# A 512-column pass for the high weight half in the feed-forward stage, with sums on drain and gate products on GpSimd

## The reference

```python
def _conv_ffn(h, w_up, conv_w, conv_b, w_down):        # D_MODEL 1024, D_FF 2816
    a, g = jnp.split(h @ w_up, 2, axis=-1)             # w_up 1024 x 5632
    a = causal_depthwise_conv(a, conv_w, width 3) + conv_b
    return (jax.nn.gelu(a) * g) @ w_down               # w_down 2816 x 1024
# and around it, in first_block:
h = _rmsnorm(x, norm_g[l, 2]) * (1.0 + sc2) + sh2
y = _conv_ffn(h, ...)
x = x + g2 * _rmsnorm(y, norm_g[l, 3])
```

## Time and profile before

| what | value |
|---|---|
| executions | 752.69, 753.12 and 759.79 us, median 753.12 |
| profiled execution | span 757.1 us; no other time of this execution is given |
| mean granted TensorE clock | 0.990 |
| TensorE busy, matmul and weight load | 730.8 us (97%) and 710.5 us (94%) |
| VectorE, ScalarE, GpSimd busy | 524.7, 396.1, 104.3 us |
| DMA | 141.13 MB, mean 186 GB/s |
| up chunks | 239.6 to 364.4 us of the span |
| down chunks | 364.4 to 426.7 us of the span |

### The profile page before, as it was taken

How to read it: one execution, slowest core, us unless ns; L and a number is a source line. 1 busy time by engine, 2 the same in 40 slices (tenths; PEclk the granted TensorE clock), 3 DMA queues, 4 the chain that set the end, 5 groups by cost and what they waited for, 6 DMA issues and landing times.

```text
span 757.1 us, 14222 instructions
## 1 busy us (share of the span) xinstructions
PE 730.8 (97%) x5964; PEld 710.5 (94%) x5964; DVE 524.7 (69%) x778; ACT 396.1 (52%) x560; POOL 104.3 (14%) x87
## 2 busy tenths in 40 slices
PE   8899999998899999999999999999999999999995
PEld 6799899898898999999999989899999999999995
DVE  4979888886977678777767556925576347555665
ACT  4286455545364544544544348528555456556551
POOL 0130000000522000000001130000004455443000
PEclk9999999999999999999999999979999999999998
DMA  8995567555363455654566544514446553343101
GB/s 343 411 356 190 203 268 274 193 204 219 113 244 146 167 200 190 213 178 161 204 261 233 205 138 148 207 66 168 167 154 223 184 206 117 116 159 112 57 1 56
DMA packets 22265, 141.13 MB, mean 186 GB/s; under 512 B 2389, under 2 KB 3029, under 8 KB 6458
## 3 DMA queue, kind: packets, MB, share of 16 engines
q1 hardware_dynamic: 21626, 137.28, 50.1%
q0 software_dynamic: 576, 2.95, 1.0%
HBM read 139.17 MB, written 1.05 MB: 185 GB/s over the span
## 4 chain that ended last, share of the span: by engine, by line
PE 70%; DVE 13%; issue 7%; ACT 5%; DMA 3%; POOL 0%; SPq 0%; DVEq 0%; ACTq 0%
PE res L1596 20%; PE res L1598 19%; PE res L1597 19%; ACT whi L639 3%; DVE wlo L1052 3%; PE pX L1803 2%; DMA shared<-in_w_ada 1%; PE pS L1783 1%; PE pX L1982 1%; DVE shared L1065 1%; DVE raw L1065 1%; DMA y<-in_w_ada 1%; ACT sq L654 1%; PE pT L1793 1%; PE pS L1644 1%
## 5 line engine op out<-in xcount | busy, mean ns | idle before, releaser
L1596 PE MATMUL res<-hhi,whi 128*128 128x256 f32 (+1 forms) x1120 | 318.9, 285 | 4.1 <-DVE wlo L1052 1.5
L1052 DVE TENSOR_TENSOR wlo<-raw,whi 128x2048 fp32r<-128x2048 f32 (+3 forms) x101 | 229.1, 2270 | 126.4 <-ACT whi L639 126.2
L1597 PE MATMUL res<-hhi,wlo 128*128 128x256 f32 (+1 forms) x1120 | 312.9, 279 | 0.0
L1598 PE MATMUL res<-hlo,whi 128*128 128x256 f32 (+1 forms) x1120 | 312.8, 279 | 0.0
L639 ACT ACTIVATE whi<-raw 128x2048 fp32r<-128x2048 f32 (+3 forms) x101 | 188.3, 1865 | 120.2 <-issue 87.1
L1596 PEld LDWEIGHTS res<-hhi,whi 128*128 128x128 f32 (+1 forms) x1120 | 209.6, 187 | 5.9 <-issue 3.4
L1597 PEld LDWEIGHTS res<-hhi,wlo 128*128 128x128 f32 (+1 forms) x1120 | 209.4, 187 | 0.4
L1598 PEld LDWEIGHTS res<-hlo,whi 128*128 128x128 f32 (+1 forms) x1120 | 209.4, 187 | 0.2
L538 POOL TENSOR_TENSOR sq<-sq,rope 128x512 f32<-128x512 f32 x18 | 39.5, 2195 | 78.5 <-ACT sq L654 78.5
L1596 PE MATMUL res<-uhi,whi 128*128 128x256 f32 x176 | 49.3, 280 | 0.0
L1597 PE MATMUL res<-uhi,wlo 128*128 128x256 f32 x176 | 49.1, 279 | 0.0
(11 more groups left out here) (334 smaller groups left out, 1211.1 us busy)
## 6 DMA issues: line engine op xcount, KB each, us to landing
raw<-in_wts SPq DMA_DIRECT2D x97, 1024.0 KB, 5.0
raw<-in_w_ada SPq DMA_DIRECT2D x16, 1024.0 KB, 5.1
shared<-in_w_ada SPq DMA_DIRECT2D x6, 1024.0 KB, 11.1
gates<-in_wts SPq DMA_DIRECT2D x4, 768.0 KB, 13.3
raw<-in_wts SPq DMA_DIRECT2D x4, 768.0 KB, 5.6
y<-in_w_ada SPq DMA_DIRECT2D x2, 1024.0 KB, 9.2
x<-in_xT SPq DMA_DIRECT2D x2, 512.0 KB, 4.7
gv<-in_ln_rows POOLq DMA_DIRECT2D x1, 1024.0 KB, 7.5
```

What stands on the lines that cost most here:

```text
L1052: nc.vector.tensor_tensor(lo[:, 0:b], raw[RAW_OF["w", c] % RAW][:, 0:b], hi[:, 0:b].bitcast(f32), ALU.subtract).then_inc(lo_ready, 1)
L1596: mm(out, ah, bh, start=first, stop=False)
L1597: mm(out, al, bh, start=False, stop=False)
L1598: return mm(out, ah, bl, start=False, stop=last)
```

## The change

Four things are changed, and all belong to the feed-forward stage.

- `hhi` and `hlo` become the two halves of one tile `hh` of [128, 8, 2, 256], and `uhi` and `ulo` those of `uh`. High and low of a k-tile lie side by side. `side_by_side` issues one matmul of the high weights with all 512 columns, and one of the low weights with the 256 high columns. The result has two parts of 256 columns for each half `i`, in two banks for a chunk. There are three such pairs of banks: `pT`, `res0` with `res1`, and `pS`. The last half of the last down block keeps `three`.
- The two parts are added on drain: ScalarE copies one part to SBUF ahead of `high`, and VectorE adds the other from PSUM ahead of `low`.
- The gate product and the subtraction for `ulo` move from VectorE to GpSimd. The rounding to `uhi` moves one iteration later on ScalarE, behind the next `high`.
- `turned` ahead of `UP + 2` is left out.

```diff
-        hhi = sb("hhi", [P, KT, T], f32r)
-        hlo = sb("hlo", [P, KT, T], f32r)
+        hh = sb("hh", [P, KT, 2, T], f32r)
+        hhi, hlo = hh[:, :, 0, :], hh[:, :, 1, :]
...
+        pairs = (pT[:, :].rearrange("p (a b) -> p a b", a=2), banks[:, 0:2, :], pS[:, :].rearrange("p (a b) -> p a b", a=2))
...
@@ GpSimd, iteration c
+                if UP <= c - 1 < DOWN and (c - 1 - UP) % 2 == 1:
+                    j = (c - 1 - UP) // 2
+                    g = gelu[:, j % 2, :, :]
+                    pool.wait_ge(gelu_done, j + 1)
+                    pool.wait_ge(drained_dve, RESULT_DRAIN[FIRST_RESULT[c - 1]][1])
+                    nc.gpsimd.tensor_tensor(g, g, gsum[:, j % 2, :, :], ALU.mult).then_inc(u_full, 1)
+                    pool.wait_ge(u_hi, j + 1)
+                    nc.gpsimd.tensor_tensor(ulo[:, 2 * j:2 * j + 2, :], g, uhi[:, 2 * j:2 * j + 2, :].bitcast(f32),
+                                            ALU.subtract).then_inc(u_lo, 1)
@@ ScalarE, iteration b
                 if b == DOWN:
                     load_root()
+                if UP <= b < DOWN:
+                    ...
+                    if (b - UP) % 2 == 0:
+                        nc.scalar.activation(aseq[:, j % 2, :, 2:T + 2], pair[:, :, 0:T], ACT.Copy).then_inc(part_copied, 1)
+                    else:
+                        nc.scalar.activation(gsum[:, j % 2, :, :], pair[:, :, T:2 * T], ACT.Copy).then_inc(part_copied, 1)
+                if DOWN <= b < GK and (b - DOWN) % 3 == 2:
+                    for i in range(1 if b == GK - 1 else 2):
+                        result(FIRST_RESULT[b] + i)
+                        nc.scalar.activation(down_sum((b - DOWN) // 3, i), pairs[pair_index(b)][:, i, T:2 * T], ACT.Copy
+                                             ).then_inc(part_copied, 1)
                 if b not in LATE and ...:
                     high(c + 2)
...
+                if UP <= b < DOWN and (b - UP) % 2 == 1:
+                    act.wait_ge(conv_done, j + 1)
+                    nc.scalar.activation(gelu[:, j % 2, :, :], conv[:, j % 2, :, :], ACT.Gelu_apprx_tanh).then_inc(gelu_done, 1)
+                if UP < b <= DOWN and (b - UP) % 2 == 0:
+                    j = (b - UP) // 2 - 1
+                    act.wait_ge(u_full, j + 1)
+                    nc.scalar.activation(uhi[:, 2 * j:2 * j + 2, :], gelu[:, j % 2, :, :], ACT.Copy).then_inc(u_hi, 1)
@@ VectorE, iteration b
+                if UP <= b < DOWN:
+                    dve.wait_ge(part_copied, parts_copied(b))
+                    ...
+                    nc.vector.tensor_tensor(part, other, part, ALU.add).then_inc(drained_dve, 1)
+                if DOWN <= b < GK and (b - DOWN) % 3 == 2:
+                    for i in range(1 if b == GK - 1 else 2):
+                        dve.wait_ge(part_copied, parts_copied(b, i))
+                        part = down_sum(j, i)
+                        nc.vector.tensor_tensor(part, pairs[pair_index(b)][:, i, 0:T], part, ALU.add).then_inc(drained_dve, 1)
                 if b not in LATE and ...:
                     low(c + 2)
@@ TensorE
+            def pair_of(c):
+                if c == UP + 1:
+                    pe.wait_ge(drained_act, RESULT_DRAIN[FIRST_RESULT[UP - 1]][1])
+                if c >= UP + 3:
+                    r = FIRST_RESULT[before_in_pair(c)]
+                    pe.wait_ge(drained_dve, RESULT_DRAIN[r + results_of(before_in_pair(c)) - 1][1])
+                return pairs[pair_index(c)]
+
+            def side_by_side(ps, ah, al, both, first, last):
+
+                mm(ps, ah, both.rearrange("p s t -> p (s t)"), start=first, stop=False)
+                return mm(ps[:, 0:T], al, both[:, 0, :], start=False, stop=last)
...
                     if c == UP:
-                        fm_first(c, hhi, hlo, lambda k: pe.wait_ge(*in_low("n3", k)), ARRIVAL)
+                        fm_pair(c, c + 2, lambda k: pe.wait_ge(*in_low("n3", k)), ARRIVAL)
                     elif c > UP + 1:
-                        if c == UP + 2:
-                            turned(c)
-                        fm(c, hhi, hlo)
+                        fm_pair(c, c + 1)
...
-                            last = three(ps[:, 0:T], wh[:, k, i * P:i * P + P], wl[:, k, i * P:i * P + P],
-                                         uhi[:, kk, :], ulo[:, kk, :], kk == 0, kk == FT - 1)
+                            ah, al = wh[:, k, i * P:i * P + P], wl[:, k, i * P:i * P + P]
+                            if j == 3 and i == 1:
+                                last = three(pair[:, i, 0:T], ah, al, uhi[:, kk, :], ulo[:, kk, :], kk == 0, kk == FT - 1)
+                            else:
+                                last = side_by_side(pair[:, i, :], ah, al, uh[:, kk, :, :], kk == 0, kk == FT - 1)
```

More of the change, by code:

```diff
@@ L122 @@
     FIRST_RESULT.append(len(RESULT_MARK))
-    for _i in range(results_of(_c)):
+    for _who in drainers_of(_c):
         _m += 1
         RESULT_MARK.append(_m)
-        _n[drainer_of(_c)] += 1
-        RESULT_DRAIN.append((drainer_of(_c), _n[drainer_of(_c)]))
+        _n[_who] += 1
+        RESULT_DRAIN.append((_who, _n[_who]))
     if not results_of(_c):
@@ L134, with pair_index, before_in_pair, parts_copied @@
 CHUNK_MARK[GOUT + 2] = CHUNK_MARK[GOUT + 3]
+def pair_index(c):
+    return (c - UP if c < DOWN else 22 + (c - DOWN) // 3) % 3
+def before_in_pair(c):
+    return c - 3 if c < DOWN else DOWN - 3 + (c - DOWN) // 3 if c < GK - 3 else DOWN + 2
+def parts_copied(c, i=0):
+    return c - UP + 1 if c < DOWN else 23 + 2 * ((c - DOWN) // 3) + i
 STREAM = []
@@ L296, in build @@
         with ExitStack() as st:
-            uhi = sb("uhi", [P, FT, T], f32r, at=st)
-            ulo = sb("ulo", [P, FT, T], f32r, at=st)
+            uh = sb("uh", [P, FT, 2, T], f32r, at=st)
+            uhi, ulo = uh[:, :, 0, :], uh[:, :, 1, :]
             aseq = sb("aseq", [P, 2, 2, T + 2], at=st)
@@ L346, in build @@
             olo = sb("olo", [P, KT, T], f32r, at=st)
-        res = [ctx.enter_context(nc.psum_tensor(f"res{i}", [P, 512], f32)) for i in range(NB)]
+        banks = ctx.enter_context(nc.psum_tensor("res", [P, NB, 512], f32))
+        res = [banks[:, i, :] for i in range(NB)]
         pS = ctx.enter_context(nc.psum_tensor("pS", [P, 1024], f32))
@@ new lines, in _ @@
+                    dve.wait_ge(drained_dve, RESULT_DRAIN[FIRST_RESULT[b]][1])
+                    if j == 0:
+                        dve.wait_ge(pad_set, 7)
+                    if j >= 2:
+                        dve.wait_ge(gelu_done, j - 1)
+                    for i in range(2):
+                        f = 2 * j + i
+                        a, o = aseq[:, j % 2, i, :], conv[:, j % 2, i, :]
+                        own(nc.vector.tensor_scalar(o, a[:, 0:T], col("conv_w", f), col("conv_b", f), ALU.mult, ALU.add))
+                        own(nc.vector.scalar_tensor_tensor(o, a[:, 1:T + 1], col("conv_w", FT + f), o, ALU.mult, ALU.add))
+                        ins = nc.vector.scalar_tensor_tensor(o, a[:, 2:T + 2], col("conv_w", 2 * FT + f), o,
+                                                             ALU.mult, ALU.add)
+                        if i:
+                            ins.then_inc(conv_done, 1)
+                        else:
+                            own(ins)
@@ L1639, in fm, with fm_pair, at @@
                         half()
+            def pair_of(c):
[8 more added lines that the diff above has]
+                return mm(ps[:, 0:T], al, both[:, 0, :], start=False, stop=last)
+            def fm_pair(c, c_end, ready=None, order=range(KT)):
+                for d in range(c, c_end):
+                    wait_weights(d)
+                pair = [pair_of(d) for d in range(c, c_end)]
+                def at(n, d, i, k):
+                    wh, wl = weights_of(d)
+                    last = side_by_side(pair[d - c][:, i, :], wh[:, k, i * P:i * P + P], wl[:, k, i * P:i * P + P],
+                                        hh[:, k, :, :], n == 0, n == KT - 1)
+                    if n == KT - 1 and i:
+                        last.then_inc(product_done, 1)
+                if ready:
+                    for n, k in enumerate(order):
+                        ready(k)
+                        for d in range(c, c_end):
+                            for i in range(2):
+                                at(n, d, i, k)
+                else:
+                    for i in range(2):
+                        for n, k in enumerate(order):
+                            at(n, c, i, k)
             def warm(n, of=ident, to=pS[:, 512:640]):
@@ L1933, in _ @@
                     kt = kt_of(c)[0]
-                    r = 2 * j + FIRST_RESULT[DOWN]
+                    pair = pair_of(c) if kg == 0 else pairs[pair_index(c)]
                     for i in range(2):
-                        ps = bank(r + i) if kg == 0 else res[(r + i) % NB]
                         for k in range(kt):
```

98 lines of the change are left out of this document (42 added, 56 removed).

## The result

| kernel | executions | median | lowest to highest |
|---|---|---|---|
| before | 20 | 753.57 us | 750.75 to 760.56 us |
| after | 20 | 760.06 us | 758.69 to 762.22 us |

The ratio on record is 1.0071 with an interval of 1.0048 to 1.0093 (it isn't the quotient of the two medians, which is 1.0086): slower, where the forecast was 745.6 us. One execution of the kernel before (2524.36 us) and one of an experiment (1022.03 us, at a granted clock of 0.65) were disturbed and are left out of all times here.

A forecast was written before the change was run, and what follows sets the result against it. TensorE's matmul stream was taken as the bound. Terms -9.9 - 0.4 + 2.0 + 0.8 = -7.5 us, put on the median of 753.1, gave 745.6 us; range 740.5 to 756.0.

The forecast's parts named there:

- The long pass at 215.9 ns, -9.9 us: Up and down chunks: 512-column pass 215.9 ns, short one 117.7, k-tile 19.5 ns less, 506 tiles, -9.9 us.
- the rival "by the column": Up and down chunks: loss grows with columns, long pass 235 ns, only costs left, +2.4 us, 755.5 us; chance 0.15.
- The base, 753.1 us: Whole kernel: difference put on the median 753.1 us, 4.0 us under the profiled execution with its half-clock stretch.
- `turned`, -0.4: Ahead of the third up chunk: three matmuls from 250.98 to 251.34 us go away, -0.4 us.
- Drains covered, 0: Up chunks, steady state: splits end about 5 us before TensorE needs them, so two-part drains cost 0.
- GpSimd's holds: Up chunks: GpSimd and VectorE instructions exclude each other, up to 2.5 us more VectorE time per pair, 0 in steady state.
- The rival "VectorE as the bound": Up chunks: GpSimd's holds stretch a pair's VectorE loop to 12.7 us, making 768 us; chance 0.08.
- The hand-over, +2.0: Up to down chunks: TensorE waits for GpSimd's late subtraction after the last gelu, +2.0 us.
- The end of the down chunks, +0.8: Last down block: VectorE's addition stands behind `low`, the last square comes some 1.3 us later, +0.8 us net.

The follow-up runs named there:

- the second and third pair: Changed kernel, last pair's products on VectorE: long passes 759.87 us, short 758.56; then also two f32 matmuls and `turned` before the third up chunk: 760.48 and 755.40.
- the insertion that gives the 340 pace: Kernel before with two f32 matmuls put directly ahead of the three transposed matmuls of `turned` at the third up chunk: 753.76 us, ratio 0.9948.

## Why the prediction was wrong, step by step

**The long pass at 215.9 ns, -9.9 us: this step failed.** It took its value from a plain float32 record of the same length. Measured are 234 ns, and 230 at best, 232 by doubling it: the rival "by the column", to which I gave 0.15; the pass lies at or over that rival's threshold of 230 ns. Against the same rhythm before, the term is 0, or -0.5 us with the 118 long tiles behind the hand-over at 349. My first argument against it, 339 ns for the value chunks, was the quicker rhythm of the same matmuls: three times 113.3. I read it as the effect of turned roles, but the same chunks run in either rhythm. In the profile of the lower group they take 11.6 / 33 = 352 ns:

```profile
L1596 PE MATMUL res<-whi,hhi x34: 281/281/282, 456.1 to 467.7; 128*128 128x256 f32 x34
```

My second, that float32 loses less on a longer pass, doesn't carry over to fp32r.

**The base, 753.1 us: failed as well,** and decided the size. I put the difference of 4.0 us between span and median on the stretch at half clock. It was the rhythm: 353 in the profile, 340 by its group in the median's execution. Against the profile's own 759.0 us, the measured terms (-0.5, -0.4, +0.7 and +0.5) give 759.3; the profiled execution after took 759.19, the median is 760.06. Against the lower group the change loses 506 x (349 to 353 - 340), 4.5 to 6.7 us. In three of five executions, then, it took a k-tile of 340 ns and gave back 349 or 353.

**`turned`, -0.4:** stands as a count of matmuls; its removal alone made no difference that was measured.

**Drains covered, 0:** held. No wait of TensorE on a split in the up chunks after.

**GpSimd's holds:** held. Groups of the kernel after, as in the earlier trace rows:

```profile
L622 POOL TENSOR_TENSOR gelu<-gelu,gsum 128x512 f32<-128x512 f32 x11 | 34.4, 3131 | 50.7 <-ACT gelu L896 50.7
L624 POOL TENSOR_TENSOR uh<-gelu,uh 128x512 fp32r<-128x512 f32 x11 | 30.9, 2808 | 16.0 <-ACT uh L901 16.0
L1394 DVE TENSOR_SCALAR conv<-aseq,cols 128x256 f32<-128x256 f32 x22 | 17.9, 812 | 0.4
```

3.13 and 2.81 us are the length beside a split, and the convolution's first instruction rose from 0.41 to 0.81 us: 22 x 0.40 = 8.8 us of VectorE's time, 0.8 a pair and not the 2.5 that I allowed. The rival "VectorE as the bound" didn't come by this way.

**The hand-over, +2.0:** the mechanism was right, the size was not. Lines of ScalarE, GpSimd and TensorE after:

```profile
370.80 0.63 ACT L896 ACTIVATE gelu<-conv 128x512 f32<-128x512 f32 x1 [3.64 <-DVE conv L1396]
...
374.80 0.61 ACT L901 ACTIVATE uh<-gelu 128x512 fp32r<-128x512 f32 x1
```

```profile
375.49 2.87 POOL L624 TENSOR_TENSOR uh<-gelu,uh 128x512 fp32r<-128x512 f32 x1 [1.30 <-ACT uh L901]
```

```profile
377.59 0.28 PE L1709 MATMUL res<-uh,wlo 128*128 128x256 f32 x1
378.42 0.50 PE L1708 MATMUL res<-uh,whi 128*128 128x512 f32 x1 [0.55 <-POOL uh L624]
```

T is 364.9 us here. Gelu starts at T + 5.9 (forecast 6.4), GpSimd ends at T + 13.5 (14.0). But TensorE, no faster than before, wants it only at T + 12.8 and not T + 12.0, and loses 0.7 us (of it 0.55 shown as the wait). What I left out is that it breaks the stream: the pace changes right there in four profiles (353 to 349 in the kernel after; 349 to 353 with `turned` back; 340 to 353 with short passes, and 340 to 353 at the 0.3 us wait for a split). In the three profiles of the second and third pair that have no wait there, it doesn't change.

**The end of the down chunks, +0.8:** held in form. VectorE's addition and ScalarE after:

```profile
427.66 0.42 DVE L1306 TENSOR_TENSOR gsum<-res,gsum 128x256 f32<-128x256 f32 x1
```

```profile
428.83 0.36 ACT L913 ACTIVATE sq<-res 128x256 f32<-128x256 f32 x1
429.10 0.46 ACT L916 ACTIVATE y<-res,pcol 128x256 f32<-128x256 f32 x1
429.99 0.47 ACT L697 ACTIVATE rstd<-pX,cols 128x256 f32<-128x256 f32 x1 [0.42 <-PE pX L1805]
```

The last down product ends near 427.5 and the root activation starts at +2.5 us, as forecast (+2.6). But the next products start 7.6 us after the end and 7.1 before: +0.5 us.

**How the 7 us divide:** with the insertion that gives the 340 pace, the kernel before has 753.76 us, the drains and GpSimd's ten pairs bring 755.40 (+1.6, where the rhythm lost at the hand-over is up to 1.8), and the long passes 760.48 (+5.1). The first two were run on separate occasions beside medians of 758.9 and 752.9 us of the kernel before, its lower groups 0.8 us apart, so the +1.6 is good to about 1 us; the +5.1 is from kernels run side by side. What decides between 230 and 234 ns in a kernel with long passes, and why the chip has these rhythms at all, stays open.

## What to carry to other kernels

Read the period of a stream from at least two executions before costing an edit in it: if the times fall in groups, find the group of your profile and count from its own time. Don't price an fp32r pass by a float32 one: here fp32r passes cost by the column, so two short passes merged into a long one save nothing, and the drain of two parts is pure cost. On a long TensorE-bound stream, look at each small interruption, since it can change the pace of all that follows; and before adding work to an engine with spare share, close its loop on paper with the waits in it.

## What the chip showed that was not expected

- A stream of fp32r matmuls of 256 columns at full clock runs at 113.3 or at 117.8 ns each, and keeps the one or the other over more than 1,400 matmuls.
- The three transposed matmuls of `turned`, 0.35 us, flip it: out of 113.3 at nine of nine places of the feed-forward, out of 117.8 at seven of eight. Two f32 matmuls (nine places) and a single plain one (nine places) left it at 117.8 ns.
- A 512-column fp32r pass takes 230 to 234 ns; its best k-tile is 349 ns where short passes reach 340.
- A late start can change the rhythm, from 0.30 us instead of 0.11 behind the one before up to a wait of 1.2 us; the rhythm that a stream starts in differs from execution to execution behind the same wait of 0.8 us.
